# Recurrence of a two-block transformer kernel: three groups' transposes together, then the first products of the inverses, with state products between them

## The reference, cut to what matters

```python
def _rwkv7_step(S, inp):
    r, w, k, v, kk, b = inp
    sa = jnp.einsum('bhvk,bhk->bhv', S, kk)
    S = S * w[:, :, None, :] - sa[..., None] * b[:, :, None, :] + v[..., None] * k[:, :, None, :]
    return S, jnp.einsum('bhvk,bhk->bhv', S, r)

def _rwkv_bidir(rin, S0_f, S0_b):
    r, decay, kd, v, kk, bd = rin
    S_f, y_f = lax.scan(_rwkv7_step, S0_f, (r, decay[:, :, 0], kd[:, :, 0], v, kk, bd[:, :, 0]))
    S_b, y_b = lax.scan(_rwkv7_step, S0_b, (r, decay[:, :, 1], kd[:, :, 1], v, kk, bd[:, :, 1]),
                        reverse=True)
    return S_f, S_b, y_f + y_b
```

## Time and profile before

| | |
|---|---|
| median of 3 runs | 4757.26 us (4755.92 to 4757.38) |
| the profiled execution's own time | 4744.87 us |
| its span, first to last instruction | 4743.1 us |
| mean granted TensorE clock | 0.940 |
| PE / DVE / ACT / POOL busy, of the span | 86% / 58% / 33% / 32% |
| instructions recorded | 105248 |

### The profile page before, as it was taken

The page is one execution under the profiler, slowest core; times in us unless marked ns, Lnnn a source line. Parts: engine busy times, 40 slices in busy tenths (PEclk is TensorE's granted clock), DMA queues, the critical chain, the costliest instruction groups (busy, mean ns, idle before and its releaser), DMA issues. The chain is left out here.

```text
span 4743.1 us, 105248 instructions
## 1 busy us (share of the span) xinstructions
PE 4102.1 (86%) x43986; PEld 3151.5 (66%) x43986; DVE 2756.3 (58%) x4726; ACT 1549.2 (33%) x2721; POOL 1498.3 (32%) x1210
## 2 busy tenths in 40 slices
PE   6999888869989799888886999599679889978898
PEld 4878688836657587678874667488436677853566
DVE  3465455556657357545556665755657656557565
ACT  1333232325542133222224552200356420025542
POOL 2233143411004323324432013655132145514213
PEclk8999999979999899899998999699899999989899
DMA  6455533261235545643324134433312443340324
GB/s 195 154 176 190 167 83 83 60 219 33 62 93 173 156 152 202 201 118 83 83 79 123 46 78 168 149 111 104 122 35 66 126 163 100 104 142 7 83 64 175
DMA packets 502686, 560.45 MB, mean 118 GB/s; under 512 B 97532, under 2 KB 397084, under 8 KB 500180
## 3 DMA queue, kind: packets, MB, share of 16 engines
q1 hardware_dynamic: 374676, 475.93, 32.2%
q10 hardware_dynamic: 127616, 78.95, 5.7%
HBM read 366.75 MB, written 192.23 MB: 118 GB/s over the span
## 5 line engine op out<-in xcount | busy, mean ns | idle before, releaser
L1096 PE MATMUL pr_acc<-hH,pr_wh 128*128 128x512 f32 (+1 forms) x1288 | 482.4, 375 | 0.0
L1097 PE MATMUL pr_acc<-hL,pr_wh 128*128 128x512 f32 (+1 forms) x1288 | 466.1, 362 | 0.0
L1098 PE MATMUL pr_acc<-hH,pr_wl 128*128 128x512 f32 (+1 forms) x1288 | 465.6, 361 | 0.0
L2660 ACT ACTIVATE an_p<-an_p,an_stat 128x1280 f32<-128x1280 f32 (+5 forms) x372 | 339.7, 914 | 162.0 <-DVE an_stat L2738 156.5
L2600 PE MATMUL an_t<-ident,an_p 128*128 128x128 f32 x2152 | 318.5, 282 | 40.5 <-ACT an_pT L2667 28.1
L2600 PEld LDWEIGHTS an_t<-ident,an_p 128*128 128x128 f32 x2152 | 235.8, 141 | 164.1 <-issue 68.0
L2693 POOL TENSOR_TENSOR an_kl<-an_k,an_kh 128x1280 fp32r<-128x1280 f32 (+3 forms) x36 | 78.5, 2181 | 833.6 <-DVE an_qh L2718 833.6
L2734 DVE CUSTOM_DVE_ANT_0 an_p<-an_s,an_mask 128x256 f32<-128x256 f32 (+8 forms) x308 | 274.8, 892 | 99.5 <-PE an_s L2583 67.1
L2091 POOL TENSOR_TENSOR rk_ml<-rk_g,rk_lmask 128x256 f32<-128x256 f32 x300 | 210.7, 729 | 357.7 <-PE rk_ps L1812 357.0
L1465 POOL TENSOR_TENSOR sp_sl<-sp_w,sp_sh 128x512 fp32r<-128x512 f32 x172 | 246.0, 1437 | 196.4 <-DVE sp_sh L1540 177.9
L2625 PE MATMUL an_oacc<-an_pT,an_v 128*64 128x512 f32 (+3 forms) x1224 | 297.9, 561 | 4.0 <-DVE an_pT L2745 1.9
(11 more groups left out here) (386 smaller groups left out, 10011.3 us busy)
## 6 DMA issues: line engine op xcount, KB each, us to landing
CHK<-ri_out SPq DMA_DIRECT2D x24, 1920.0 KB, 8.0
rk_in<-CHK SPq DMA_DIRECT2D x120, 384.0 KB, 6.5
pr_w<-in_w_in ACTq DMA_DIRECT2D x58, 512.0 KB, 3.9
UT<-pr_out SPq DMA_DIRECT2D x45, 640.0 KB, 4.3
sp_w<-in_w_in ACTq DMA_DIRECT2D x50, 512.0 KB, 5.1
U<-sp_c SPq DMA_DIRECT2D x100, 256.0 KB, 2.0
mod_w<-in_w_mod SPq DMA_DIRECT2D x16, 1024.0 KB, 7.9
mo_w<-in_w_out SPq DMA_DIRECT2D x16, 1024.0 KB, 10.2
```

The source lines that it names most:

```text
L1096: nc.tensor.matmul(out, wh[:, u, k, 0:m], hi, start=(k == 0), stop=False)
L1097: nc.tensor.matmul(out, wh[:, u, k, 0:m], lo, start=False, stop=False)
L1098: ins = nc.tensor.matmul(out, wl[:, u, k, 0:m], hi, start=False, stop=(k == KT - 1))
L2660: nc.scalar.activation(row, row, ACT.Exp, bias=stat[:, n % NPM, j, 1:2], scale=heads[groups[n][0]].scale, accum_out=total[:, n % 4, j:j + ...
```

## The change

On TensorE, block b's order goes from T0 S0 T1 S1 T2 S2 st0 bv0 st1 bv1 bv2 to T0 T1 T2 S0 S1 st0 S2 bv0 st1 bv1 bv2 (st0 and st1 belong to block b - 1 and are missing for b = 0). On ACT the copies go from T0 S0 T1 S1 T2 S2 to T0 T1 T2 S0 S1 S2. DVE, POOL and SP are as before, and no wait is added or removed.

```diff
@@ -1911,13 +1911,13 @@
                 for b in range(NB):
                     before, more = b > 0, b + 1 < NB
                     turned(b, 0)
+                    turned(b, 1)
+                    turned(b, 2)
                     start_t(b, 0)
-                    turned(b, 1)
                     start_t(b, 1)
-                    turned(b, 2)
-                    start_t(b, 2)
                     if before:
                         state(b - 1, 0)
+                    start_t(b, 2)
                     bv(b, 0)
                     if before:
                         state(b - 1, 1)
@@ -1986,6 +1986,7 @@
                 for b in range(NB):
                     for g in range(NP):
                         turned(b, g)
+                    for g in range(NP):
                         start_t(b, g)
                     for g in range(NP):
                         bv(b, g)
```

## The result

The changed kernel is slower: 4777.09 us (median of 8 runs, 4768.13 to 4782.47) against 4757.32 us (8 runs, 4750.25 to 4764.54) of the kernel before, ratio 1.0038 with a 95% interval of 1.0028 to 1.0048, or +13 to +23 us. The forecast was 4764 in a range of 4752 to 4776; on the 4757.26 it was made against, the ratio gives 4775.3, just inside the range; the median itself lies 1 us above it. Between them the difference is 30.1 us.

The account below looks back on a forecast made before the run. TensorE was taken to bound the recurrence, with stops for late code pages. Steps 1 to 4 (-1 us) and Step 5 (+8) gave +7: 4752 us on the profiled execution, 4764 on the medians, range 4752 to 4776.

Parts of the forecast that it names:

- Step 2: T2 must wait for DVE's copy of T0, until about +2.25 us from T0's start: cost 0.45 us a block.
- steps 1 and 2: T0 to st0: fewer changes between transposes and 64x64 matmuls gain 0.53 us a block; T2's uncovered wait costs 0.45.
- step 3: S2 placed behind st0: nothing waits for it before the level loop, so cost zero.
- Step 4: First block of each layer, without state products: S2 and bv0 wait for ACT's copies, about +0.3 us, twice.
- Step 5: TensorE's code pages are entered later in the block, so next pages and stops come later: +8 us, bounds 0 to 13.
- the seven: Blocks with page entry at instructions 114 to 162: entered 0.95 us later, next stop's end 0.3 us later each, 2.1 us.
- each passed on whole: Every delay of a page entry reaches the following stops in full: 6.4 + 6.7 = 13 us.
- rival (b): Late page entries delay stops in state product and loop's first round one to one: 4770 to 4773 us, chance 0.18.
- 8 lie where nothing changes: Eight of 20 blocks, page entry up to instruction 27 or from 177 on: no change forecast.
- The rival of the wait: In the experiments' forecasts: T2's wait is the cost; covering it gives -5 to 0 us against the kernel before.

Follow-up runs that it names:

- the first experiment: S2 alone moved behind st0 (T0 S0 T1 S1 T2 st0 S2, ACT as before), against the kernel before: ratio 1.0001, -5 to +6 us.

## Why the prediction was right or wrong

**Direction and main cause: right.** The reorder gains nothing where TensorE runs freely, and it loses through code that comes late. Step 2 came out within 0.03 us (T2 at +2.28), and steps 1 and 2 together as forecast (st0 at +4.26, W at +9.09; in the last block of layer two W came 0.1 us sooner than before). For step 3 the first experiment shows no cost. Step 4 was too small: from T0 to W the two first blocks of a layer took 0.56 and 0.37 us longer, where I had 0.2. The direction wasn't a confident call, though: I gave 0.53 to a change within 0.2% and 0.37 to a slower kernel, and it is 0.4% slower.

**Size: wrong by more than half.** +18 us against +7. Step 5 fails in two places, and a term is missing.

First, "the seven, with a mean of 8.45, would go to 8.75: 0.3 each". I took the spread of returns under the loads for a cushion, and read it from three blocks. In the six of the seven that show this stop in both profiles, its end goes from a mean of +8.62 to +9.41: 0.8 each, most of the 0.95 by which I had put the entry later. The seven grew by 9.2 us in all, 1.3 each. Of this, 5.1 us are stops and 2.2 us T2's wait; four of the seven also have a fall of the clock that they didn't have before. With the loads cut or moved away the medians still differed by 13.6 and 14.9 us. That is near the 13 us that I had worked out for "each passed on whole" and given to rival (b), but in part by luck: in the recurrences of the profiled executions the two orders differ by 10.5 and 8.6 us, and what differs outside them isn't explained.

Second, "8 lie where nothing changes (up to 27, or from 177 on)". These eight grew by 11.2 us between the two profiles, as much a block as the seven; 9.7 us of it are stops, and 6.3 us come from the two blocks with their entry 10 and 8 instructions in.
Third, the clock, to which the prediction gave no term. In the profiled pair it is up to 17 of the 30.6 us (an estimate, worked out above), about as much as the longer stops. How much it is in the median isn't shown: the mean granted clock of the eight runs of the changed kernel is 0.937, and of seventeen runs of before, in the experiments, 0.939, which would be up to 8 us; but the order T T T S S S, with the same loss, has 0.938. The falls stand at long stops, so I count them to what late code costs; no kernel took the two apart.

**The rival of the wait.** In my experiments I set page entries and T2's wait against each other, and neither alone fits. With S0 ahead of T2, most or all of the loss is gone (4753.64 against 4750.93, -3 to +8 us). With the loads moved this order is clearly ahead of the changed one (0.9894 against 0.9938); against the old one (0.9906) the intervals overlap. So the three T in a row with T2's uncovered wait are the cause. They cost little by the 0.45 us on TensorE, for which the saved changes of shape pay, and much by what they do to the supply of code behind them. How the loss splits between T2's wait and the three T in a row isn't shown; no kernel had the three T together without the wait, because T2 and T0 share their banks.

**The Trainium skill's rule** (Runtime: NRT & Kernel Launch, Instruction fetch mechanics) that crossing into a new block of code is mostly hidden isn't borne out here: moving the loads out of the stretch took 45 us from the run without touching TensorE's code. Its figure of 256 instructions a block is: 128 more moved the stops and 256 put them back.

## What to carry to other kernels

Where an engine's straight code is dense in short instructions, count its pages: stops marked "issue" that come every 128 matmuls point to late code, and adding 128 instructions ahead of them tells. A wait that looks free, because a gain elsewhere pays for it, can still make that code later. Look at the granted clock too before putting a difference down to idle time alone. Then keep big DMA transfers out of that stretch, and let them run while a loop that is already in the engine does the work; here that was worth 0.9%, far more than any order of the stages. And judge such a change by many runs: one profiled execution lay 12 us below its median, two thirds of the effect, and the two profiles differed by 30 us where the medians differ by 20.

## What the runs showed of the hardware

- A page of TensorE's code that is asked for while block loads fill the DMA engines comes late: there are 5 us and more from stop to stop (814.16 to 819.30 to 824.72), and in the changed order a single stop reached 2.86 us.
- The request for the next page isn't tied to the moment when a page's first matmul runs. Entries 1.37 and 1.38 us into a block were followed by packets that start in windows from +2.5 and from +3.75, the later one where three T and a wait stood behind the entry.
- In the changed kernel the granted clock fell to the 1.2 GHz level at stops of 1.7 to 2.9 us, 14 times in the first 21 us of the blocks; the 24 matmuls of a state product took 1.55 us behind one of them and 0.87 us at the 2.4 GHz level.
- The store of y (384 KB over two transfers) in the same stretch did no harm that these runs can tell.
